# Loads moved ahead of stores on the sync queue, and small matrix products taken round the four quarters of the array, in a hybrid encoder layer

## What is computed

```python
def step(S, inp):                       # RWKV-7, one token of one head, S is 64x64
    r_t, w_t, k_t, v_t, kk_t, b_t = inp
    S = (S * w_t[:, :, None, :]
         + jnp.einsum('bhvk,bhk->bhv', S, -kk_t)[..., None] * b_t[:, :, None, :]
         + v_t[..., None] * k_t[:, :, None, :])
    return S, jnp.einsum('bhvk,bhk->bhv', S, r_t)
...
scores = jnp.einsum('nbhcd,nbhmd->nbhcm', qc, kc) * decay_in      # retention, chunks of 64
inner = jnp.einsum('nbhcm,nbhme->nbhce', scores, vc)
def step(R, inp):
    q_c, k_c, v_c = inp
    cross = jnp.einsum('bhcd,bhde->bhce', q_c, R) * q_decay[None, :, :, None]
    R = R * chunk_decay[None, :, None, None] + jnp.einsum('bhmd,bhme->bhde', k_c * k_decay[None, :, :, None], v_c)
    return R, cross
```

## Time and profile before

| | |
|---|---|
| median of 3 runs | 1731.5 us (1729.8 to 1734.6) |
| the profiled execution | 1733.7 us |
| its span, first to last instruction | 1731.9 us |
| mean granted TensorE clock | 0.912 |
| busy: PE, PE weight load, DVE, ACT, POOL | 85%, 74%, 55%, 40%, 37% |
| the mixing stage | from about 464 to 1012 us |

### The profile page before, as it was taken

How to read it: one execution, slowest core, us unless ns; L and a number is a source line. 1 busy time by engine, 2 the same in 40 slices (tenths; PEclk the granted TensorE clock), 3 DMA queues, 4 the chain that set the end, 5 groups by cost and what they waited for, 6 DMA issues and landing times. The chain is left out here.

```text
span 1731.9 us, 32895 instructions
## 1 busy us (share of the span) xinstructions
PE 1479.7 (85%) x14419; PEld 1275.8 (74%) x14419; DVE 951.0 (55%) x1014; ACT 697.0 (40%) x669; POOL 632.9 (37%) x215
## 2 busy tenths in 40 slices
PE   5999999999698889888889830799999999999940
PEld 4989999999696667667668620688888888888830
DVE  5455664442144354354355341678787787778726
ACT  4442342223121121121121100677777878777712
POOL 1001110000000000000000003899999999999934
PEclk9999999999888898898998965899999999999975
DMA  5133445343392231222230178699999999999856
GB/s 182 50 119 126 148 136 171 90 130 86 110 356 95 104 96 60 104 70 86 105 97 35 38 50 293 220 401 414 414 414 413 415 413 415 413 415 414 316 196 252
DMA packets 188628, 366.59 MB, mean 212 GB/s; under 512 B 17169, under 2 KB 76864, under 8 KB 187472
## 3 DMA queue, kind: packets, MB, share of 16 engines
q1 hardware_dynamic: 175328, 318.69, 51.8%
q0 software_dynamic: 7424, 25.18, 3.8%
q10 hardware_dynamic: 5760, 20.97, 3.0%
HBM read 295.81 MB, written 69.01 MB: 211 GB/s over the span
## 5 line engine op out<-in xcount | busy, mean ns | idle before, releaser
L1057 PE MATMUL ps<-u_hi,w_hi 128*128 128x352 f32 (+1 forms) x720 | 239.6, 333 | 6.9 <-DVE u_lo L708 6.9
L1057 PE MATMUL ps<-u_lo,w_hi 128*128 128x352 f32 (+1 forms) x720 | 235.3, 327 | 0.0
L1057 PE MATMUL ps<-u_hi,w_lo 128*128 128x352 f32 (+1 forms) x720 | 234.3, 325 | 0.0
L2398 POOL TENSOR_TENSOR down_lo<-down_raw,down_hi 128x1024 fp32r<-128x1024 f32 x32 | 178.6, 5581 | 31.4 <-ACT down_hi L2443 31.4
L2398 POOL TENSOR_TENSOR gate_lo<-gate_raw,gate_hi 128x1024 fp32r<-128x1024 f32 x32 | 177.3, 5540 | 6.5 <-ACT gate_hi L2443 6.5
L2526 DVE TENSOR_TENSOR down_lo<-down_raw,down_hi 128x3072 fp32r<-128x3072 f32 x32 | 109.4, 3420 | 97.1 <-ACT down_hi L2443 97.1
L2398 POOL TENSOR_TENSOR up_lo<-up_raw,up_hi 128x1024 fp32r<-128x1024 f32 x32 | 154.8, 4838 | 1.6 <-ACT up_hi L2443 1.0
L1057 PEld LDWEIGHTS ps<-u_hi,w_hi 128*128 128x128 f32 x720 | 138.9, 193 | 13.9 <-issue 10.6
L1057 PEld LDWEIGHTS ps<-u_lo,w_hi 128*128 128x128 f32 x720 | 138.8, 193 | 0.0
L1057 PEld LDWEIGHTS ps<-u_hi,w_lo 128*128 128x128 f32 x720 | 138.8, 193 | 0.0
L2443 ACT ACTIVATE gate_hi<-gate_raw 128x4096 fp32r<-128x4096 f32 x32 | 116.5, 3641 | 53.0 <-SPq L2341 53.0
(11 more groups left out here) (379 smaller groups left out, 3190.5 us busy)
## 6 DMA issues: line engine op xcount, KB each, us to landing
gate_raw<-in_moe_w_gate SPq DMA_DIRECT2D x32, 2048.0 KB, 12.4
up_raw<-in_moe_w_up SPq DMA_DIRECT2D x32, 2048.0 KB, 14.2
down_raw<-in_moe_w_down SPq DMA_DIRECT2D x32, 2048.0 KB, 12.8
tm_rows<-tm_stage SPq DMA_DIRECT2D x32, 512.0 KB, 3.3
y_slots<-y_out ACTq DMA_DIRECT2D x32, 512.0 KB, 6.8
w_raw<-in_w_in SPq DMA_DIRECT2D x30, 512.0 KB, 3.7
tm<-tm_rows SPq DMA_DIRECT2D x8, 1792.0 KB, 8.7
fm<-fm_rows SPq DMA_DIRECT2D x8, 1024.0 KB, 6.7
```

Of the source, the lines that this page charges most:

```text
L1057: mm = pe.matmul(z_of(n, r_), w[n % 3][:, k_, :], a[:, k_, c0:c1], start=(k_ == 0 and i == 0), stop=(k_ == KD - 1 and i == 2))
L2398: pool.tensor_tensor(lo[e % 2][:, cut:, :], raw[e % 2][:, cut:, :], hi[:, cut:, :].bitcast(F32), ALU.subtract).then_inc(sem(f"{name}_lo2_r ...
```

## The change

On SP, the loads of q to kr and of v to rg of tile t + 1 go ahead of the residual stores of tile n, to the place where the a to r rows were loaded, and ahead of these; the wait for `mixed_b_ready` goes with them. On TensorE, `cross`, `to_features` and the step at L2074 go round the four quarters of the array in the order (0,0), (1,1), (0,1), (1,0); in the accumulating call of `to_features` the second product of a pair comes after a round of four. `advance`, `ret_scores`, `ret_inner` and `ret_cross` alternate between two quarters or two halves at each product. No product, transfer or wait is added or taken away.

```diff
@@ -1346,15 +1346,14 @@
 
                     if t + 1 < NT:
                         sp.wait_ge(sem("rz_t_ready"), n)
+                        sp.wait_ge(sem("mixed_b_ready"), n)
                         sp.wait_ge(sem("y0_done"), n)
+                        load_fm(t + 1, "q", "kr")
+                        load_tm(t + 1, "v", "rg")
                         load_fm(t + 1, "a", "r")
                     store_h2(n)
                     load_h(t)
                     store_u2(n)
-                    if t + 1 < NT:
-                        sp.wait_ge(sem("mixed_b_ready"), n)
-                        load_fm(t + 1, "q", "kr")
-                        load_tm(t + 1, "v", "rg")
                 store_h2(NTX)
                 store_u2(NTX)
                 sp.wait_ge(sem("h2_stored"), 16 * NTX)
@@ -1744,33 +1743,35 @@
                                                start=(n == 0), stop=(n == len(pairs) - 1))
                     return mm
 
+
+                QUARTERS = ((0, 0), (1, 1), (0, 1), (1, 0))
+
                 def cross(banks, at_, lhs, rhs):
 
-                    for a in range(2):
-                        for q in range(4):
-                            for c in range(2):
-                                f = slice(q * P + c * C, q * P + (c + 1) * C)
-                                mm = pe.matmul(ps[c * C:(c + 1) * C, banks + a, at_ + q * C:at_ + (q + 1) * C],
-                                               lhs[a * C:(a + 1) * C, f], rhs[a * C:(a + 1) * C, f], start=True, stop=True)
+                    for q in range(4):
+                        for a, c in QUARTERS:
+                            f = slice(q * P + c * C, q * P + (c + 1) * C)
+                            mm = pe.matmul(ps[c * C:(c + 1) * C, banks + a, at_ + q * C:at_ + (q + 1) * C],
+                                           lhs[a * C:(a + 1) * C, f], rhs[a * C:(a + 1) * C, f], start=True, stop=True)
                     return mm
 
                 def to_features(banks, pairs, ends=True):
 
 
-                    for c in range(2):
-                        p_ = slice(c * C, (c + 1) * C)
-                        for h in range(HA):
-                            a, q = h % 2, h // 2
-                            f = slice(h * C, (h + 1) * C)
-                            for n, (lhs, rhs) in enumerate(pairs):
+                    for q in range(4):
+                        for n, (lhs, rhs) in enumerate(pairs):
+                            for c, a in QUARTERS:
+                                h = 2 * q + a
+                                p_ = slice(c * C, (c + 1) * C)
+                                f = slice(h * C, (h + 1) * C)
                                 mm = pe.matmul(ps[a * C:(a + 1) * C, banks + c, q * C:(q + 1) * C], lhs[p_, f], rhs[p_, f],
                                                start=(n == 0 and (ends or q == 0)), stop=(ends and n == len(pairs) - 1))
                     return mm
 
                 def advance(bank, m, st):
-                    for a in range(2):
-                        p_ = slice(a * C, (a + 1) * C)
-                        for q in range(4):
+                    for q in range(4):
+                        for a in range(2):
+                            p_ = slice(a * C, (a + 1) * C)
                             f = slice(q * C, (q + 1) * C)
                             mm = pe.matmul(ps[p_, bank, f], m[p_, f], st[p_, f], start=False, stop=(q == 3))
                     return mm
@@ -1896,8 +1897,8 @@
                 def ret_scores(t):
                     pe.wait_ge(sem(f"fm_q_loaded{t % 2}"), 16 * ((t + 1) // 2))
                     q_t, kr_t = feat(t, "q"), feat(t, "kr")
-                    for c in range(2):
-                        for h in range(HB):
+                    for h in range(HB):
+                        for c in range(2):
                             f = slice(h * P + c * C, h * P + (c + 1) * C)
                             mm = pe.matmul(ps[c * C:(c + 1) * C, 3, h * C:(h + 1) * C], kr_t[:, f], q_t[:, f], start=True, stop=True)
                     mm.then_inc(sem("scores_done"), 1)
@@ -2067,13 +2068,12 @@
                     pe.wait_ge(sem("state1_ready"), t)
                     pe.wait_ge(sem("rz_t_ready"), t)
                     advance(5, m_t[:, 1, :], state[1])
-                    for a in range(2):
-                        p_ = slice(a * C, (a + 1) * C)
-                        for q in range(4):
-                            for c in range(2):
-                                mm = pe.matmul(ps[c * C:(c + 1) * C, 2 + a, 256 + q * C:256 + (q + 1) * C],
-                                               rz_t[p_, q * P + c * C:q * P + (c + 1) * C],
-                                               state[c][p_, q * C:(q + 1) * C], start=True, stop=True)
+                    for q in range(4):
+                        for a, c in QUARTERS:
+                            p_ = slice(a * C, (a + 1) * C)
+                            mm = pe.matmul(ps[c * C:(c + 1) * C, 2 + a, 256 + q * C:256 + (q + 1) * C],
+                                           rz_t[p_, q * P + c * C:q * P + (c + 1) * C],
+                                           state[c][p_, q * C:(q + 1) * C], start=True, stop=True)
                     mm.then_inc(sem("y1_done"), 1)
 
                 pe.wait_ge(sem("consts_loaded"), 16)
```

## The result

The changed kernel takes 1652.4 us (median of 4 runs, 1643.8 to 1656.6) against 1730.7 for the kernel before: a ratio of 0.955, 95% interval 0.950 to 0.960. The forecast was 1656, with a range of 1638 to 1688.

What follows compares the result with a forecast made beforehand. TensorE was taken to set the pace of a tile, waiting for loads queued behind stores. 40.0 + 24.4 + 22.3 - 11.4 = 75.3 us off 1733.7 gave 1658.4, against the median 1656, range 1638 to 1688.

Steps and rivals of the forecast that it cites:

- The stalls: TensorE's waits for the q and kr load (33.4 us) and the `tm` load (6.6) in tiles 2 to 7: 40.0 us gone.
- The clock: From retention scores to feature products in six tiles, half clock after TensorE stood still would go: 24.4 us gained.
- the unthrottled length of the stretch: Scores to first feature product at full clock: 1.97 us to L1893 (tile 1) plus 7.02 from there (tile 6), together 8.99.
- The orders: Small TensorE products going round quarters or halves of the array start closer together: 2.9 us a tile, 1.95 in the last, 22.3 gained.
- The prediction's argument on the bank: L1743 alternates row halves in one bank at 28 ns, half of one quarter's 56, so `advance` and L1915 would gain too.
- The gain of the cross products in the prediction: In `cross`, 96 records a tile would start 19 ns apart where it was 23: 0.38 us a tile.
- Instruction fetch: At a tile's start, instructions arriving late behind longer data traffic: 11.4 us lost, between bounds of nothing and 32.
- Program order: Rival: matmuls start and end strictly in program order, so orders gain 0.6 us a tile instead of 2.9: 1674, chance 0.12.
- one bank: Rival: different row tiles cannot access one PSUM bank at once, so `advance` and L1915 gain nothing: 1665, chance 0.04.
- the low clock that stays: Rival: thin 64x64 work, not the stall, keeps the clock down, so the clock gain is lost: 1680, chance 0.08.
- took the stall's place: Rival: another wait (x_p or w_m of VectorE, late u2) takes half of the stall's place, 20 us: 1676, chance 0.06.
- The slower case: Rival: fetch starves; four fetches a tile 2.7 late, doubled by the clock, lose 130 us over six tiles: 1775, chance 0.03.

Runs made afterwards that it cites:

- experiment 1: The kernel before with only the three loads moved ahead of the residual stores, every product in its old order: 1674.0 us, ratio 0.970.
- Experiment 4: The kernel before with useless products filling TensorE's wait ahead of the retention scores: 1726.4 us, ratio 0.999; with both load waits filled: 1715.1 us, ratio 0.992.
- the late version: The changed kernel with one more wait on SP, so the three loads are issued some 13 us into a tile: 1638.2 us, ratio 0.947.
- experiment 2: The changed kernel with SP's old order of loads, so only the orders of products are new: 1698.9 us, ratio 0.985.
- experiment 5: The changed kernel with loads later (1638.2 us) or an extra 1792 KB transfer (1656.9 us); the kernel before with late loads and old orders (1656.8 us).
- experiments 2 and 3: The second: the kernel before with loads moved and only part of the new orders, four-quarter ones 1662.0 us, two-quarter or two-half ones 1660.5 us.

## Why the prediction was right

**The stalls, 40.0 us.** Right: cross to scores fell by 33.4, and from tile 2 on no wait for a load is left. That it agrees to the tenth is in part luck, since this part holds the gain of the cross products and the late instructions too; in experiment 1's trace it fell by 34.6. The passed stores delayed no product: from tile 2 to 8 TensorE waits for no transfer at all.

**The clock, 24.4 us.** The sum of the two terms, 64.4, fits (the first three parts fell by 65.3 us in experiment 1's trace), its split was not right. The step that failed is the unthrottled length of the stretch, 1.97 + 7.02: I put all above it and above the visible 6.6 down to the clock. Experiment 4 gives 15.2 to the clock (57.3 to 42.1) and 9.2 to the landing of the `tm` load, which no faster clock would have brought forward. Whoever had trusted the 24.4 and kept the clock up without moving the loads would have gained 14 us with two fillings and nothing with one.

**The orders, 22.3 us.** They are worth 27 (21 to 32). The mechanism held; the size of `to_features` was off (17 ns a record, where I took the middle of 14 and 24, 19), the cross products stand 15 ns apart where nothing disturbs them (96 in 1.63 us in the late version), and with them the last part of a tile lost the half clock that experiment 1 still had. `advance` came at 31 ns and L1916 and L1923 at (1.09 - 0.27) / 15 = 55, near my 28 and 56. The prediction's argument on the bank, that one quarter allows a record each 56 ns, disagrees with its own 49 for L1775; the outcome does not hang on it. I split them 10 to 12 between four and two quarters; measured is 15 and 18 on top of the loads, each give or take 9. Tile 8, where I counted 1.95, gave 1.7 in the changed kernel and 2.1 in experiment 2. The gain of the cross products in the prediction, 0.38 a tile, is not to be seen in the changed kernel: cross to norm is 204.2 for 203.8 before. It is there in the kernel with the orders alone (197.2, of which a part is that one tile fewer ran into the half clock), and was eaten by the next term.

**Instruction fetch, 11.4 us lost.** Right in sign and near in size; the mechanism, instructions that come late behind data, is borne out by experiment 5, but I priced it by the traffic alone. By the traffic alone it is nothing to be seen (203.0 for 203.8 with the old orders); with the new orders the same loads cost 204.2 - 197.2 = 7.0 us in the stretch (known to some 3), and the waits without a cause rose by 9.6 us over the stage. The late loads win back 0.7 points, about 13 us (the two intervals, 0.944 to 0.951 and 0.950 to 0.960, just meet), more than was lost, because they also spare what the kernel before paid. That experiment 1 came out within its 1672 to 1678 is therefore luck in part: its trace shows a loss not at the start of the tile but 4.3 us at its end, at half clock. What decides how late a transfer of instructions starts stays open.

**The rivals.** Program order (1674) and one bank (1665) fell with experiments 2 and 3; the low clock that stays (1680) fell with PEclk at 1.00. Nothing took the stall's place: x_t is ready 0.05 us before L1742 starts at 782.18, the thin cover that the prediction named. The slower case had its mechanism right and was far from its price: its trigger, waits as long as 2.7 us four times a tile, did not come (six such waits in all at the cross products, 7.6 us together), and the loss was some 7 us and not 130.

## What to carry to other kernels

On a queue that issues in order, put a load that waits for nothing ahead of a store that waits for the middle of the step, but not into the stretch where TensorE issues its smallest products: of the two places tried here the one 13 us later was the better, with 1638 us instead of 1652. Let small products change the quarter of the array at every instruction, both halves of the rows and of the columns, even within one bank. And before a slow stretch behind a stall is blamed on the clock, look at what lands in the middle of it: slow work may cover a second wait.

## What the runs showed of the hardware

- Records of 64x64 products stand 49 ns apart on one quarter, 28 to 31 on two, 15 to 17 on four, and instructions of another quarter overtake in start (the first L1754 of tile 7 starts at 799.10, ahead of the last L2074, which comes before it in the program; so in the earlier trace rows).
- Data traffic of 1 to 5 MB at the start of a tile lengthened 32 us of TensorE work by 1 to 2.7 us a tile, though no product there waited for data; with the old orders it was 2.0 us with 1 MB and 1.9 with 3.3. I had expected a loss, but not that the kernel before already paid 12 us (203.8 against 191.9) with its one early load.
- TensorE's unexplained waits end 1.2 to 1.6 us after a 16 KB transfer of the instruction queue has ended, 74 of 74, and beside a load the transfer starts later (2.9 us into tile 4 for 1.0).
- Filling both waits with useless products kept the clock at its upper level in the six stretches behind them (57.3 to 42.1 us); filling the first alone gained nothing, since the `tm` load landed no earlier.
